# Regrouping the modulation products, the value projection and the context load of a three-block transformer kernel

## The reference

```
for i in 0, 1:                                  # layers 0 and 1
    mod = silu(c) @ ada_w[i] + ada_b[i]         # 1024 x 6144: 12 chunks of 512 columns
    h = rms_norm(x, norm_mix_g[i]) * (1 + sc1) + sh1
    y = diff_attention(h) if i == 0 else chunked_attention(h)
        # q, k, v = h @ w_qkv; q and k normed per head; softmax; values; (layer 0:
        # the output normed per head too); @ w_o
    x = x + g1 * y
    h = rms_norm(x, norm_ffn_g[i]) * (1 + sc2) + sh2
    x = x + g2 * grouped_moe(h)                 # router, top 2 of 16 experts
# block 2: the same frame; the mixer is an MLP over chunks, a latent attention over
# tokens and a context, and a two-way gated scan; then 32 experts
```

## Time and profile before

| | |
|---|---|
| runs, us | 1628.68, 1630.15, 1632.28 (median 1630.15) |
| profiled execution, us | 1626.78 |
| its span from first to last instruction, us | 1625.0 |
| PE busy | 1567.5 us, 96% |
| DVE busy | 565.6 us, 35% |
| ACT busy | 395.4 us, 24% |
| POOL busy | 52.0 us, 3% |
| read from memory | 533.48 MB, 329 GB/s over the span |

### The profile page before, as it was taken

The page is one execution under the profiler, slowest core; times in us unless marked ns, Lnnn a source line. Parts: engine busy times, 40 slices in busy tenths (PEclk is TensorE's granted clock), DMA queues, the critical chain, the costliest instruction groups (busy, mean ns, idle before and its releaser), DMA issues.

```text
span 1625.0 us, 21285 instructions
## 1 busy us (share of the span) xinstructions
PE 1567.5 (96%) x8521; PEld 898.1 (55%) x8521; DVE 565.6 (35%) x1346; ACT 395.4 (24%) x861; POOL 52.0 (3%) x65
## 2 busy tenths in 40 slices
PE   6989999999999999999999999889999999999998
PEld 3654675445456747644545876567645445454454
DVE  2555432322235272432222265442332312223122
ACT  1242321112122432411211253352311112111121
POOL 0000010000000001000000034001000000000000
PEclk9999979999999999999999999799899999999999
DMA  9998749999998778599999400521599999999995
GB/s 355 341 333 317 304 206 420 428 429 428 429 383 293 287 282 323 228 429 428 428 430 415 170 0 2 208 104 45 230 427 426 429 428 428 429 428 428 429 427 223
DMA packets 94820, 535.23 MB, mean 329 GB/s; under 512 B 7952, under 2 KB 11882, under 8 KB 70195
## 3 DMA queue, kind: packets, MB, share of 16 engines
q1 hardware_dynamic: 94354, 534.39, 80.9%
q10 hardware_dynamic: 416, 0.17, 0.0%
HBM read 533.48 MB, written 1.06 MB: 329 GB/s over the span
## 4 chain that ended last, share of the span: by engine, by line
PE 85%; DMA 9%; DVE 2%; ACT 1%; SPq 1%; issue 1%; POOL 0%; DVEq 0%; POOLq 0%; ACTq 0%
PE pair L1024 26%; PE bank L1011 7%; PE pair L1031 6%; PE bank L755 6%; PE bank L1031 6%; DMA ring<-in_w_dram 5%; PE bank L1073 3%; PE pair L1073 3%; PE pair L1101 3%; PE bank L652 2%; PE bank L849 2%; PE pair L731 2%; DMA arena<-in_b_s_dram 1%; PE bank L762 1%; PE bank L1101 1%; DMA ring<-in_a_w_qkv_dram 1%
## 5 line engine op out<-in xcount | busy, mean ns | idle before, releaser
L1024 PE MATMUL pair<-ring,arena 128*64 128x512 f32 x2048 | 447.4, 594 | 1.0 <-DMA ring<-in_w_dram 1.0
L1024 PEld LDWEIGHTS pair<-ring,arena 128*64 128x64 f32 x2048 | 144.3, 137 | 285.9 <-issue 285.5
L2350 DVE TENSOR_TENSOR arena<-sq,pair 128x512 f32<-128x512 f32 x32 | 33.9, 1060 | 388.8 <-PE pair L1024 388.8
L1011 PE MATMUL bank<-arena 128*128 128x128 f32 x1120 | 140.7, 281 | 3.2 <-DVE arena L2232 3.2
L1011 PEld LDWEIGHTS bank<-arena 128*128 128x128 f32 x1120 | 134.9, 197 | 3.5 <-issue 3.4
L1031 PE MATMUL pair<-ring,arena 128*64 128x512 f32 x512 | 116.9, 598 | 0.0
L755 PE MATMUL bank<-hh,ring 128*128 128x256 f32 x512 | 115.1, 382 | 1.1 <-DMA ring<-in_a_w_qkv_dram 1.1
L1031 PE MATMUL bank<-ring,arena 128*64 128x512 f32 x512 | 115.3, 592 | 0.0
L1706 ACT ACTIVATE sq<-pair 128x512 f32<-128x512 f32 x32 | 19.1, 597 | 366.9 <-PE pair L1024 366.9
L755 PEld LDWEIGHTS bank<-hh,ring 128*128 128x128 f32 x512 | 95.8, 190 | 21.1 <-issue 6.8
L2358 DVE COPY arena<-bank 128x512 f32<-128x512 f32 x32 | 22.1, 692 | 181.1 <-PE bank L1031 181.1
(11 more groups left out here) (408 smaller groups left out, 1724.5 us busy)
## 6 DMA issues: line engine op xcount, KB each, us to landing
ring<-in_w_dram SPq DMA_DIRECT2D x96, 2048.0 KB, 15.7
ring<-in_moe_w_gate_dram SPq DMA_DIRECT2D x32, 2048.0 KB, 11.9
ring<-in_moe_w_up_dram SPq DMA_DIRECT2D x32, 2048.0 KB, 16.6
ring<-in_moe_w_down_dram SPq DMA_DIRECT2D x32, 2048.0 KB, 14.8
ring<-in_ada_w_dram SPq DMA_DIRECT2D x24, 2048.0 KB, 17.3
ring<-in_w_mod_dram SPq DMA_DIRECT2D x12, 2048.0 KB, 11.9
ring<-in_a_w_qkv_dram SPq DMA_DIRECT2D x6, 2048.0 KB, 20.5
ring<-in_b_w_qkv_dram SPq DMA_DIRECT2D x6, 2048.0 KB, 16.8
```

The source lines that it names most:

```text
L1011: last = mm(b[part][:, cols(k % 4)], h_tok[:, t, cols(k)], pick_n[:, t, :], start=(t == 0), stop=(t == TT - 1))
L1024: last = mm(b[2 + m][half(a), :], x_sel[:, k, half(a)], R8[moe_slot(l, a, m)][:, k, :], start=(k == 0), stop=(k == KT - 1))
L2350: tt(hid.rearrange("p (f q) -> p q f", f=FT), by_row(gate_act), by_row(b[3]), ALU.mult).then_inc(M["hid_ready"], 1)
```

## The change

The PE list of both attention layers:
- `mods(A[0])` and `mods(A[1])` go from behind the four query projections to behind the first and the second of them. The position product (L875) stays behind the fourth.
- `sums(10)` goes ahead of `mods(A[2])`.
- `values_in(21, 5, 1)` goes ahead of `mods_turn`, `spread(0, 1)`, `mods(B[0])` and `spread(1, 1)`, right behind `values_in(20, 5, 0)`.
- In layer 0 `out_spread(1)` goes ahead of `router_row` and `mods_turn(3)`, and on DVE `out_normed(1)` ahead of `mods_add(3)` and `route_weights`.

The split of the modulation: chunks 4, 5, 20 and 21 (A[0] and A[1] of both layers) have n=3 instead of n=0. Chunks 12, 28 and 14 (B[0] of both layers, B[2] of layer 0) leave the dictionary: eight products each, and no `weighted_rows`.

SP: in layer 1's experts `load_hybrid` is issued ahead of the two up matrices instead of ahead of the two down matrices.

```diff
@@ experts (SP) @@
                 for m in range(3):
-                    if l == 1 and m == 2:
+                    if l == 1 and m == 1:
                         load_hybrid()
@@
-        PRODUCTS = {4: 0, 5: 0, 6: 3, 7: 3, 11: 3, 12: 3, 13: 3, 14: 3, 20: 0, 21: 0, 22: 3, 23: 3, 28: 3, 29: 3, 30: 3}
+        PRODUCTS = {4: 3, 5: 3, 6: 3, 7: 3, 11: 3, 13: 3, 20: 3, 21: 3, 22: 3, 23: 3, 29: 3, 30: 3}
@@ attention_layer (PE) @@
                 close_values(l)
-                for i in range(2, 6):
-                    project(i, 0)
+                project(2, 0)
+                mods(A[0])
+                project(3, 0)
+                mods(A[1])
+                project(4, 0)
+                project(5, 0)
                 if l == 0:
                     mm(b[5][0:8, :], t5b, bucket, start=True, stop=True).then_inc(t5_ps, 1)
-                mods(A[0])
-                mods(A[1])
                 for i in range(6, 10):
                     project(i, 2)
-                mods(A[2])
                 if l == 0:
                     pe.wait_ge(table_in, 16)
                 sums(10)
+                mods(A[2])
                 mods(A[3])
@@
                 values_in(20, 5, 0)
+                values_in(21, 5, 1)
                 mods_turn(2 * l + 2)
                 spread(0, 1)
                 mods(B[0])
                 spread(1, 1)
-                values_in(21, 5, 1)
                 if l == 0:
                     out_spread(0)
                 mods(B[1])
@@
                 out_first(7)
+                if l == 0:
+                    out_spread(1)
                 router_row(l)
                 mods_turn(2 * l + 3)
-                if l == 0:
-                    out_spread(1)
@@ attention_layer (DVE) @@
-                weighted_rows(B[0])
                 mods_add(2 * l + 2)
                 normed(0, 1)
                 normed(1, 1)
                 weighted_rows(B[1])
-                weighted_rows(B[2])
+                if l == 1:
+                    weighted_rows(B[2])
                 if l == 0:
                     out_normed(0)
@@
                 half_out(7)
+                if l == 0:
+                    out_normed(1)
                 mods_add(2 * l + 3)
                 route_weights(l)
-                if l == 0:
-                    out_normed(1)
```

## The result

| | before | after |
|---|---|---|
| median of 5 runs, us | 1630.15 (1627.9 to 1632.28) | 1639.48 (1638.37 to 1641.52) |
| ratio, 95% interval | | 1.0062 (1.0045 to 1.0078) |
| span of the profiled execution, us | 1625.0 | 1637.7 |
| granted clock, profiled execution | 0.974 | 0.976 |
| PE busy, us | 1567.5 | 1576.9 |

The account below looks back on a forecast made before the run. The prediction took PE as the bound, 85% of the chain. Its terms, 1.85 + 0.85 + 4.1 + 7.0 + 3.4 - 3.8 - 0.7, gave +12.7 us on the median 1630.15: 1642.8 us, range 1636 to 1649.

Parts of the forecast that it names:

- step 4: Both value products ahead of the spread leave DVE's chain behind mods_turn uncovered: +4.1 us layer 0, +7.0 layer 1, plus clock.
- Step 1, the split.: Modulation split: more products on PE for A[0] and A[1] cost +0.85 us in each attention layer.
- Step 2, the position row.: Layer 0, first part: mods between projections delay the position row's store and the loads behind it, +1.85 us at a projection.
- the bound of 3.5: Upper bound for the position row's delay, if the longer wait for A[5] makes a second stretch at half clock.
- Step 3.: sums(10) ahead of mods(A[2]): the spread starts as long after the last projection as before, 0 us.
- Step 4, the clock.: PE falls to half clock in the gaps behind mods_turn: 1.7 us per layer, +3.4 in all, bounds 0 and 6.8.
- Step 5.: End of layer 0's attention: earlier out_spread(1) saves 2.1 us of waiting and 1.7 of half clock, -3.8 us.
- Step 6.: Layer 1's route: context loads issued first shorten PE's wait, limited by ACT's copying, -0.7 us.
- The split does what it looks meant for: Rival, chance 0.06: slots freed earlier bring A[5] and QKV 1 in time; +7.3 us in all, 1637.5.
- faster, by the clock: Rival, chance 0.03: PE stays warm through both routes and the value-product gaps, 15 us back; -5.7 us, 1624.5.
- twice the half clock: Rival, chance 0.12: value-product gaps cost two half-clock stretches each, the wait for A[5] one more; +17.8 us, 1648.
- the gaps stay warm: Rival, chance 0.10: no half-clock loss of 3.4 us in the value-product gaps; +9.3 us, 1639.4.

Follow-up runs that it names:

- e4: The kernel before with only mods(A[0]) and mods(A[1]) between the query projections, three products each instead of none: 1635.68 us, ratio 1.0045.
- e11: e9 with the split of A[0] and A[1] put back as in before, both behind the fourth projection: 1619.23 us, ratio 0.9944.
- e9: e1 with the position product moved behind the first query projection, as in e5: 1620.06 us, ratio 0.9947.
- e5: e4 with the position product behind the first query projection and ACT copying its row right after the first query: 1629.28 us, ratio 0.9997.
- e10: The kernel before with only the position product behind the first query projection and ACT's copy behind the first query: 1625.89 us, ratio 0.9971.
- e1: The changed kernel with the second value product back behind the spread of the keys: 1627.28 us, ratio 0.9991.
- e2: The kernel before with only the second value product moved ahead of mods_turn and the spreads: 1643.72 us, ratio 1.0102.
- e6: The changed kernel with DVE's weighted rows of B[1] (layer 1 also B[2]) ahead of mods_add and the normed queries: 1631.13 us, ratio 1.0014.
- e3: The kernel before with only layer 0's out_spread(1) ahead of router_row and mods_turn(3), and its DVE work likewise: 1626.96 us, ratio 0.9990.
- e12: e11 with block 2's three context loads back ahead of the down matrices, as in before: 1621.49 us, ratio 0.9951.
- e7: The kernel before with only block 2's three context loads moved ahead of the up matrices: 1632.10 us, ratio 1.0012.

## Why the prediction was right, and where its sizes were off

The verdict and the sign were right: slower by over 0.2%, 1639.48 inside 1636 to 1649. The sum of 12.7 us is also the difference of the two spans, but that is luck: step 4 came out 2.7 us below its price and 1.0 came off in stretches that no step priced, while steps 1, 2 and 6 came out 0.3, 1.8 and 1.6 us above theirs.

- **Step 1, the split.** +0.85 per layer; the first part of layer 1 showed +1.2 in after and in e4, e11 against e9 1.2 back. Slightly low. The Trainium skill, TensorEngine Tiling (Array Packing), Overview, gives up to 4x for 32 columns, by which the split would have cost nothing; these +1.2 us do not agree with that.
- **Step 2, the position row.** The mechanism was exact: store at 68.60 (said 68.2), A[5] at 91.79 (91.9), the projection at 97.30 (97.4). The size was 3.6, not 1.85: the second wait grew to 2.73 us and the projection behind it ran at a clock of 0.50. That is the size of the bound of 3.5 that I had named and not taken, but one instruction later than I named it: behind the longer wait for A[5] its products ran at full speed (1.92 us for 3.42), and the time that this saved went into the wait for the load. e5 and e10 show that the row is the cause.
- **Step 3.** Zero, as said: the sums waited 0.84 for ACT's square and the spread 0.69 where it had waited 1.55.
- **Step 4.** Without the clock +4.1 and +7.0, measured +5.0 and +6.8; e1, e2 and e6 each show the mechanism. One detail was wrong: the wait does not stand ahead of all of `mods(B[1])`. In the changed kernel its three ordinary products went ahead and only the product with ones waited, 0.63 us in layer 0 and 4.28 in layer 1 where I said 2.9 and 5.3. DVE sets the end, so the sum is the same.
- **Step 4, the clock.** This is the term that was mis-sized: 3.4 taken, about 0.9 found, all in layer 0 (0.50 at 160 to 164 in the stretches below). In layer 1 the clock fell too, 0.59 at 599 to 603, but PE was waiting for DVE's second set of rows at the time: scores(5) started 14.5 us behind `mods_turn`, as DVE alone has it. A slow clock under a wait is free, and I had not applied that to my own term. One of the two rows from which I took its size was itself such a case: from the store of the row to the projection it took 29.2 us in before, with A[5] at 3.42 us, and 28.9 in e2, with A[5] at 1.92. It is not always free: in e2's layer 1 the same products ran slow and outlasted DVE, whose add was done at 606.83, and scores(5) started at 607.58, 15.2 us behind `mods_turn`.

```profile
160.00:164.00 4.00, 3.37 (x11) 0.35 (x8) 3.89 (x8) 0.00 (x0) 0.00 (x0) 0.50 1.05 387
...
599.00:603.00 4.00, 3.42 (x13) 1.17 (x16) 3.86 (x6) 0.00 (x0) 0.00 (x0) 0.59 1.08 347
```

- **Step 5.** -3.8 said and -3.9 in the trace (sc5 to ss); by the timing of e3 alone -1.6, with an interval from -4.1 to +1.0.
- **Step 6.** -0.7 said. The products behind ACT's copies started 11.7 us later than before where the stage had started 12.1 later: -0.4. But the sums of squares behind them ran slower (6.51 us for 5.15), so the stage as a whole came out at +0.9. The step priced the wait alone and not the clock behind it: the twelve other kernels, set out under e12, have 24.3 to 25.4 us for this stage with the early context, and 24.9 or 26.8 to 27.7 without it.
- **From profile to median.** Adding the same 12.7 to the median was the step that put the forecast 3.3 us above the measured 1639.5. The profiled execution of before lay 3.4 below its median, that of after (1639.51) on it. A difference between two single executions carries that scatter; the medians differ by 9.3.
- **The rivals.** "The split does what it looks meant for" and "faster, by the clock" fell. Of "twice the half clock" one more stretch did come in the first part of layer 0, though behind the wait for QKV 1 and not at A[5]; the part in step 4 did not. That leaves "the gaps stay warm", +9.3 and 1639.4, which comes out at the measured median, but not by its mechanism: the clock did fall in the gaps.

## What to carry to other kernels

A long product between an engine's short steps can be the cover of a serial chain on another engine: before moving it ahead, add up the chain from its new start, and ask what the other engine could do in the idle time that the move makes; e6 got back 7.8 of 10.1 us with DVE's list alone. Where one queue issues all loads, look for the wait in it that is not for a buffer: one small product placed earlier (e10) was worth 4.7 us, while the split, which frees the slots earlier, cost 7.3 (e4). And price a clock loss only where the matrix engine has work that nobody else holds up.

## What the runs showed of the hardware

- Half clock after short gaps: in after PE idled 2.30 us ahead of A[5], worked 2.8 us and idled 2.73, and the projection then took 5.38 us for 3.69, at a clock of 0.50 to 0.65. In e4, with 2.46 and 2.74 idle around the same work, it took 5.21. In e2, e3 and e7, with 1.46 to 1.65 and the same 2.73, it took 3.69. So the length of the last gap alone doesn't decide. For A[5] itself even the order is reversed: behind 1.78 idle it took 3.42 us (before), behind 2.30 and 2.46 it took 1.92 (after, e4). The Trainium skill, TensorE: Matmul & The Clock Gate, Part 1, says that how much runs slow at the start varies between runs of the same kernel. Up to this point before, e2, e3 and e7 run the same code on PE, and A[5] took 3.42 us in the first and 1.92 in the other three, behind 1.46 to 1.65 idle; that agrees with the page, but as the idle times differ too it doesn't prove it.

```profile
93.68 3.69 PE L755 MATMUL bank<-hh,ring 128*128 128x256 f32 x16 [2.73 <-DMA ring<-in_a_w_qkv_dram]
```

That is e2's line; after's, above, has the same bracket and 5.38.

- The stretch from layer 1's expert loop to block 2's is the same code in all kernels and took from 482.6 us (after) to 488.2 (e12). In e7 (488.1) its clock is 1.00 for the first 300 us and falls to 0.66 in one stretch of 25 us in block 2's mixers. So the spans of two single profiles can differ by over 5 us without any change in the code; what a small change does is read from the starts of the instructions around it.
